# Transfers issued a stage early and the first router's search split into two halves, in a two-block transformer kernel on one Trainium2 core

## The reference, cut to what matters

```
# first block
mod = silu(c) @ w_mod + b_mod                     # six rows of 1024: shift, scale, gate, twice
u   = rmsnorm(x) * (1 + scale) + shift            # for the tokens, and for the context
p   = u @ gdn_w_in                                # q, k, v, z of 8 heads
...                                               # short conv, silu, gated delta rule in two directions
y   = (o * rsqrt(mean(o*o)) * o_gain * silu(z)) @ gdn_w_out
h   = x + gate * y
# expert choice: every one of 16 experts takes the 128 tokens that like it best
aff = softmax(u2 @ w_router)                      # 1024 x 16
gates, idx = top_k(aff.T, 128)                    # 16 x 128, over all 1024 tokens
h   = h.at[idx].add(gate_f * gates * swiglu(u2[idx]))
# second block: norms, narrow and wide projections, state-space scan, windowed attention,
# output projection with w_out_2, a router with top-2 of 32 experts, experts, final norm
```

## Time and profile before

| | us |
|---|---|
| median of 3 runs | 4617.72 |
| lowest, highest | 4614.37, 4617.97 |
| profiled execution | 4615.21 |
| span of its trace | 4613.5 |
| PE busy in the span | 4118.3 (89%) |
| DVE busy | 1541.0 (33%) |
| mean granted clock of TensorE | 0.943 of full |

### The profile page before, as it was taken

How to read it: one execution, slowest core, us unless ns; L and a number is a source line. 1 busy time by engine, 2 the same in 40 slices (tenths; PEclk the granted TensorE clock), 3 DMA queues, 4 the chain that set the end, 5 groups by cost and what they waited for, 6 DMA issues and landing times. The chain is left out here.

```text
span 4613.5 us, 42680 instructions
## 1 busy us (share of the span) xinstructions
PE 4118.3 (89%) x14684; PEld 2249.2 (49%) x14684; DVE 1541.0 (33%) x3314; ACT 815.6 (18%) x1818; POOL 400.3 (9%) x385
## 2 busy tenths in 40 slices
PE   6699999998777999999999996997798889999984
PEld 4366666666423444444444443544665344444432
DVE  4577777776352000000000004235953310000003
ACT  2223333332110000000000003111163101011002
POOL 0111111111000000000000000002500010000001
PEclk8799999999888999999999997998799989999997
DMA  6111111110467898888888874010012279999986
GB/s 270 50 27 36 41 41 36 41 30 22 167 256 294 310 313 305 304 313 309 306 308 311 308 264 147 24 29 13 1 70 87 80 254 334 334 335 334 336 312 238
DMA packets 437206, 875.43 MB, mean 190 GB/s; under 512 B 89745, under 2 KB 134625, under 8 KB 430921
## 3 DMA queue, kind: packets, MB, share of 16 engines
q1 hardware_dynamic: 410905, 785.86, 48.8%
q0 software_dynamic: 19616, 71.38, 4.6%
q10 hardware_dynamic: 6544, 16.39, 0.9%
HBM read 801.14 MB, written 72.43 MB: 189 GB/s over the span
## 5 line engine op out<-in xcount | busy, mean ns | idle before, releaser
L1707 PE MATMUL moe_gbank<-moe_ring,moe_xT 128*128 128x512 f32 x1536 | 679.9, 596 | 3.8 <-ACTq L1763 3.8
L1725 PE MATMUL moe_acc<-moe_ring,moe_hidT 128*128 128x512 f32 x1536 | 675.1, 592 | 1.8 <-DVEq L1824 1.1
L1707 PE MATMUL moe_ubank<-moe_ring,moe_xT 128*128 128x512 f32 x1536 | 675.1, 592 | 0.0
L1797 DVE TENSOR_TENSOR moe_hid<-moe_sg,moe_ubank 128x512 f32<-128x512 f32 x96 | 66.0, 688 | 1632.4 <-PE moe_ubank L1707 1632.4
L799 PE MATMUL gdn_pbank<-mix_xT,gdn_w 128*128 128x512 f32 (+1 forms) x1280 | 541.2, 557 | 2.6 <-PEq L693 2.6
L1707 PEld LDWEIGHTS moe_gbank<-moe_ring,moe_xT 128*128 128x128 f32 x1536 | 293.5, 191 | 373.7 <-issue 370.5
L1725 PEld LDWEIGHTS moe_acc<-moe_ring,moe_hidT 128*128 128x128 f32 x1536 | 288.2, 190 | 347.1 <-issue 347.1
L1707 PEld LDWEIGHTS moe_ubank<-moe_ring,moe_xT 128*128 128x128 f32 x1536 | 284.5, 190 | 322.4 <-issue 322.4
L1768 ACT ACTIVATE moe_sg<-moe_gbank 128x512 f32<-128x512 f32 x96 | 57.3, 597 | 1547.6 <-PE moe_gbank L1707 1547.6
L799 PEld LDWEIGHTS gdn_pbank<-mix_xT,gdn_w 128*128 128x128 f32 x1280 | 229.6, 194 | 161.3 <-issue 152.8
L2146 PE MATMUL proj_abank<-mix_yT,mix2x_wq 128*128 128x512 f32 x416 | 180.8, 592 | 0.6 <-PE proj_abank L2146 0.6
(11 more groups left out here) (523 smaller groups left out, 4769.9 us busy)
## 6 DMA issues: line engine op xcount, KB each, us to landing
moe_ring<-in_moe_w_gate SPq DMA_DIRECT2D x64, 2048.0 KB, 7.9
moe_ring<-in_moe_w_up SPq DMA_DIRECT2D x64, 2048.0 KB, 8.2
moe_ring<-in_moe_w_down SPq DMA_DIRECT2D x64, 2048.0 KB, 8.0
moe_ring<-in_w_gate SPq DMA_DIRECT2D x32, 2048.0 KB, 10.5
moe_ring<-in_w_up SPq DMA_DIRECT2D x32, 2048.0 KB, 9.8
moe_ring<-in_w_down SPq DMA_DIRECT2D x32, 2048.0 KB, 10.1
...
```

The source lines that it names most:

```text
L1707: last = nc.tensor.matmul(bank[:], xT[:, k, :], w[:, k * 512:(k + 1) * 512], start=(k == 0), stop=(k == KD - 1))
L1725: last = nc.tensor.matmul(acc[j][:], hidT[:, k, :], w[:, k * D + j * 512:k * D + (j + 1) * 512], start=(f == 0 and k == 0), stop=(f == NF ...
L1797: nc.vector.tensor_tensor(hid[:], sg[:], ubank[:], ALU.mult).then_inc(u_free, 1)
```

## The change

1. **z of head 0.** `projections(-1)` now holds also z0 and z1 of head 0; `projections(0)` no longer does.
2. **w_out of out1.** The normed input `xT` of delta_net moves to an enclosing stage "first". When z1 of head 7 is done, nobody reads `xT` any more, and SP, in iteration 7, loads the eight pieces of `gdn_w_out` into that space (`w_next`, semaphore `w_ahead`). The wait for all eight `yT_d` stores moves from delta_net's end to out1's last `yk` load. out1 loads only `yk`.
3. **Modulation pieces.** SP loads pieces 0 to 3 in out1, after the first three token tiles; the router stage loads 4 to 23 (and an anti-identity `rev` of 64 KB).
4. **The search.** `work` is 48 partitions of 512: partitions 0 to 15 hold tokens 0 to 511 for the 16 experts, 32 to 47 tokens 512 to 1023. The 16 rounds go on as they were, on both halves at once, and give 128 of each half, sorted. PE turns both lists; the second is reversed by a matmul with `rev`, and DVE takes the larger at each place, which gives the 128 largest of all, with their indices (about ten small DVE instructions).
5. **The last scatter of moe1** uses a tile of the outermost level and a semaphore `scattered`; moe1's end no longer waits for it.
6. **norms_and_narrow**: first the five loads that the context tiles need (`ctx_loaded`), then the other three rows, the wait for `scattered`, then x2, x3, `wv`, `wz`. DVE begins the context tiles after `ctx_loaded`.
7. **Tables and scan**: their five rows are loaded in `project`, into tiles of the enclosing stage.
8. **out2 and the second router**: attention's SP loads `w_out_2` (eight pieces of 512 KB) and the second router's seven rows after its own three; out2 and rt2 load neither.

The enclosing stages add blocks of semaphores that are cleared at some seams: two more after route, one after ssd, one more after rt2, while delta_net, proj and rt2 themselves have other counts by one or none.

```diff
 def projections(i):
     names = [(f"v{j}", i + 1) ...] + [(f"q{j}", i + 1) ...] if i + 1 < H else []
-    if 0 <= i < H:
-        names += [(f"z{j}", i) for j in range(2)]
+    if i != 0:
+        names += [(f"z{j}", max(i, 0)) for j in range(2)] if i < H else []
...
                         sp.dma_start(yT_d[i - 1], ...).then_inc(y_stored, 16)
+                    if i == H - 1:
+                        sp.wait_ge(p_full, P_AT["z1", i])
+                        for k in range(KD):
+                            sp.dma_start(w_next[:, k, :], w_out[k * P:(k + 1) * P, :]).then_inc(w_ahead, 16)
...
-                sp.wait_ge(y_stored, 16 * H)
...
                 for k in range(KD):
                     if yT is None:
+                        if k == KD - 1:
+                            sp.wait_ge(y_stored, 16 * H)
                         sp.dma_start(yk[:, k, :], yT_d[k]).then_inc(w_loaded[k], 16)
-                    sp.dma_start(w[:, k, :], w_out[k * P:(k + 1) * P, :]).then_inc(w_loaded[k], 16)
+                    if w_here is None:
+                        sp.dma_start(w[:, k, :], w_out[k * P:(k + 1) * P, :]).then_inc(w_loaded[k], 16)
...
+                for tile, rows, ahead in pieces:
+                    sp.dma_start(tile[:], rows).then_inc(ahead, 16)
...
-                for n in range(PIECES * KD):
+                for n in range(MOD_AHEAD, PIECES * KD):
...
                 for t in range(NT):
-                    last = nc.tensor.transpose(aT[t // 4][...], ex[:, t, :], ident)
+                    h, c = divmod(t * P, HS)
+                    last = nc.tensor.matmul(halves[32 * h:32 * h + E1, c:c + P], ex[:, t, :], ident, start=True, stop=True)
...
+                nc.tensor.matmul(cps[:, 0:2 * E1], rev[:], low[:]..., start=True, stop=True).then_inc(rev_ready, 1)
...
-                for j in range(2):
-                    nc.vector.tensor_copy(work[0][:, j * 512:(j + 1) * 512], aT[j][:])
+                nc.vector.tensor_copy(work[0][:], halves[0:HP, :])
...
+                sp.wait_ge(scattered, 16)
+                for t in range(NC_T, NB):
+                    load_x(t)
```

251 lines of the change are left out of this document (144 added, 107 removed).

## The result

| | before | after |
|---|---|---|
| median, us | 4617.78 (4614.37 to 4617.97) | 4580.52 (4566.30 to 4582.84) |
| profiled execution | 4615.21 | 4581.15 |
| span of its trace | 4613.5 | 4579.5 |

The ratio is 0.9915 with an interval of 0.9903 to 0.9927. The change takes 37.3 us; 47.8 were forecast. 4580.5 lies in the range of 4554 to 4585, 10.5 above the 4570.

The account below looks back on a forecast made before the run. PE, busy for 89% of the span, was taken as the bound, so gains had to come from stretches where it stands, mostly seams. Terms summed to -47.8 from 4615.2, 4567.4; with 2.5 for the median 4570, range 4554 to 4585.

Parts of the forecast that it names:

- z of head 0: delta_net: 13.9 us of moved matmuls fit in PE's 22.6 us wait, no gain in iteration 0; 0, bounds -5 and +13.9.
- out1: Start of out1: stage starts 2.9 us earlier and first yk lands 5.1 after its issue; -4.7, bounds -3 and -6.
- router: First router: shorter search rounds let moe1 start 13.3 us earlier; a rival, 8%, had the term near 0, 4583.
- n34: moe1's end and norms_and_narrow: no wait for the scatter, context rows first; -10.8 us, between -8 (weights) and -15 (DVE's chain).
- tabs, ssd: Tables and scan: waits for small rows at the stage starts disappear; -2.3 and -4.6 us.
- out2: Start of out2: 5.1 us wait gone, 2.4 more from PE no longer starting slow; -7.5, bounds -5 and -8.
- second router: Start of rt2: of PE's 8.4 us wait for seven rows, the 5.2 behind the stage's start go; -5.2, no clock gain.
- the early pieces: First router: four early modulation pieces give nothing; a rival, 8%, had them shorten the modulation by 10 us, 4560.
- if the early transfers fill queues that others wait for: Rival at attention's start and out1's token tiles, 3%: each seam gives half its gain, 4590.
- z was covered: Rival in delta_net, 9%: z of head 0 not hidden in PE's wait, +13.9 us, 4584.
- DVE's chain: Rival in norms_and_narrow, 10%: n34 follows it, 4 us less, 4566; with out2's and rt2's bounds 4560.
- moe1's granted clock: Rival in moe1, 2%: slower, with a mean clock of 0.97 or less instead of 0.99; at 0.95 the result is 4630.

Follow-up runs that it names:

- e3: The changed kernel with all 24 modulation pieces loaded in the router's stage, as before the change; 4580.67 us, ratio 0.9919 to the kernel before.
- e2: The changed kernel with the first router's search put back to 16 partitions of 1024; 4598.07 us, ratio 0.9955 to the kernel before.
- e4: The changed kernel without moe1's last scatter, its semaphore only raised; 4547.26 us, a total not to be read since the second router assigns other blocks.
- e7: The changed kernel with GpSimd waiting for the last scatter's landing before moe1 ends; 4579.09 us, ratio 0.9913 to the kernel before.
- e8: The changed kernel with router pieces multiplied earlier, separate wait for wz, attention's early loads behind its own three rows; 4577.29 us, ratio 0.9910 to the kernel before.
- e11: The changed kernel with router pieces multiplied earlier, separate wait for wz, attention's early loads behind the third output; 4574.64 us, ratio 0.9910 to the kernel before.
- e5: The changed kernel with z of head 0 back in iteration 0; 4579.81 us, ratio 0.9918 to the kernel before.
- e6: The changed kernel with w_out_2 loaded in out2 again, the second router's rows still in attention; 4583.00 us, ratio 0.9932 to the kernel before.
- e10: The changed kernel with attention's early loads issued only after a wait for the third output; 4580.65 us, ratio 0.9918 to the kernel before.

## Why the prediction was right, and where it was not

The sum said -47.8 and the medians say -37.3 in the first set, -46.9 and -36.3 in the two others. By terms, in the profiled executions:

| term | forecast | measured |
|---|---|---|
| z of head 0 | 0 | +1.2 to +1.7 in the first two heads (0.2 to 2.9 in all of delta_net) |
| out1 | -4.7 | -4.0 |
| router | -13.3 | -14.4 to -15.7 |
| n34 | -10.8 | -6.0 to -6.4 |
| tabs, ssd | -2.3, -4.6 | -2.35, -4.7 |
| attention | nothing | +1.7 to +3.0, or +7.3 to +7.7 |
| out2 | -7.5 | -5.1 for the wait, -0.7 for the clock |
| second router | -5.2 | -5.2 |
| extra clears | +0.6 (rt2, ssd) | not to be seen: rt2 to moe2 50.2 before, 49.5 after |

**Router: right, in each step.** Rounds of 2.24 (2.25 forecast), nothing from the early pieces (e3, and a DMA share of 0.11 just where an empty queue was forecast), and the merge behind the last piece but done before the stores were all issued. It gave 1.1 to 2.4 us more than forecast. The last piece is on PE 63.8, 64.6 and 64.9 after the stage's start in the three executions, 65.4 and 65.1 before; I did not follow that further. From the end of the stores' issue to moe1's start it was 4.4, and 4.9 was forecast. Of these, the 1.7 for the stores' landing stand on no row, before or after; only the 4.4 as a whole is measured. The cause of the gain is e2's to show: with the old search the 15 to 17 us are back.

**out1, tabs, ssd, second router: right.** Each was a first landing that stood on the path, and it left with its load. In out1 the two parts that were forecast can be seen apart: the seam fell from 5.88 to 3.53, and the first `yk` landed after 5.20 (5.1 forecast). The price by the Trainium skill (DMA: Bandwidth & Descriptors, "Anatomy of one DMA"), a fit for transfers that GpSimd issues, would have it land after 3.2, an estimate; for these, issued by SP, the traces don't agree: 5.2 to 5.3 in all twelve executions with the change.

**n34: the reordered rows were right, the wait for the scatter was not.** "Without the wait for the scatter the stage starts at 2791.2 + 1.6 = 2792.8, 7.7 earlier" is the step that failed: it took the row's 1.60 as the whole time in which the scatter holds GpSimd, and the barrier needs GpSimd. From the index copy the stage starts 10.6 to 11.0 later, and 11.9 to 12.05 before: about 1.2 earlier and not 7.7. e4 and e7 give what the scatter costs the seam, 5.4 us, and what the wait alone was worth, 1.7; GpSimd's `DRAIN`, which ends 1.4 after the landing, takes the place of the wait. The rest of the gain, 6.4 to 6.7, comes from the five rows that now stand first: DVE's first scale moved from 16.72 to 10.0 to 10.4 after the stage's start, about as forecast (7.3 of the 15 were the order's share). Of these PE gave 1.4 to 1.8 back, since it waited for all of `w_loaded` before it turned the second context tile, and `wz` now comes late: the wait of 7.35 at 2805.57. The prediction named `wz` as one of two ends, and had the wrong bounds around it, because both counted from a start that was 6.4 us too early. e8 and e11 took 2.4 of this back.

**z: the cover held, and the price came through another door.** "In iteration 0 PE's load drops by as much, but there DVE's rows of the solve fill the time, so I take no gain" was right, and nothing was asked about what a PE with less to do does to its clock. It fell to 0.64 and 0.50 where it had been 1.00, and PE's busy time in delta_net rose from 951.4 and 952.7 to 954.7 and more in the eleven executions with the move (948.0 in e5). The first two heads cost 1.2 to 1.7 us more, the whole stage 2.3 in the mean of the eleven (0 to 4.4), inside the bounds of -5 to +13.9. e5 shows that the move is the cause; that it acts by the clock is read from the rows.

**out2: the wait was right, the clock was not.** The step "a PE that starts at 3525.0 should not be slow at all: 8 x 0.30 = 2.4 more" failed. PE starts 2.34 after its last matmul instead of 7.43, and still its granted clock over the first 8 us is 0.79 (0.70 in the earlier trace rows). It gave 0.7 (e6 against the kernel after). In e10 it was 1.00, after the same pause from the same clock. So the length of the pause doesn't decide it alone.

**Attention: not forecast.** The prediction has it in one half-sentence, "if the early transfers fill queues that others wait for", as a rival with 3%. A small part of that is true: the own rows land 1.5 later (e6 against after). The larger part is a form of the stage with a slower clock, in five executions of eleven. The load doesn't hold it down: in e10 the clock was full again 21 us before the load began. The kernel before, in its two profiles, and e6 had the short form; with five long ones in eleven, three short ones in a row would come up by chance about once in six, so they don't show that the change brings the long form about. What decides it stays open: in e10 and in e4 alike the clock was at 0.71 to 0.73 over the 4 us around attention's start and at 0.50 over the 8 us after that, and e10 had the long form and e4 the short one. A mixture of both forms can move a median of the changed kernel by several microseconds, which is the size of the difference between 4570 and 4580; that it did isn't shown, since only profiled executions tell their form.

Adding up: +1.5 - 4.0 - 14.7 - 6.2 - 7.05 + 2.1 - 5.8 - 5.2 = -39.4 without the long form (tabs and ssd as one, out2's wait and clock as one). The measured -36 to -47 lie on both sides of it. Of the 9.3 us between the first two profiled executions of the kernel after, 6.0 are in the second experts, which the change doesn't touch, 2.5 in ssd and 1.8 in delta_net. That the median fell inside the range is in part luck: the n34 term was 4.6 too large and attention's cost was missing, and the router's surplus and the width of the range covered them.

**The rivals and two sums.** None of the six came about as a whole: the early pieces gave nothing, the router's term was not near 0, z was covered, n34 didn't follow DVE's chain, most seams gave their whole gain, and moe1's granted clock over 1376 us is 0.99 before and after, with PE busy for 1365.0 and 1363.9. Two numbers of the prediction don't follow from its own terms. "Ends of the terms added: -34 to -62" counts z's -5 in the one end and leaves its +13.9 out of the other; with it that end is -20. And 57 us lost in moe1 by PE at half clock are a mean clock of 0.95 (1365 x 0.99 / 1422), not 0.97. Neither changed the forecast.
